# Moving the first attention's output normalisation into its loop, and opening the second projection half on 384 of 512 tokens

## The reference

```python
def per_block(qb):                       # 128 queries; NSA heads
    p_c = masked_softmax(s_c, cmp_end[None, :] <= tq[:, None])   # 31 compressed keys
    p_s = masked_softmax(s_s, ...)       # all selected keys
    p_w = masked_softmax(s_w, m_w)       # window
...
o = g[..., 0:1] * o_c + g[..., 1:2] * o_s + g[..., 2:3] * o_w
o = head_rms_norm(o, out_g.reshape(Hn, D))        # o * rsqrt(mean(o*o) + eps) * g, per head of 64
y_nsa = o.reshape(B, T, NSA_WIDTH) * jax.nn.silu(gate)
...
# memory group: softmax over 256 memory keys, head_rms_norm, silu gate
x = x + concat([y_rwkv, y_nsa, y_mem], -1) @ w_out[l]
```

## Time and profile before

| | |
|---|---|
| median of 3 runs | 1946.72 us |
| profiled execution, its own time | 1947.26 us |
| profiled execution, span | 1945.3 us |
| PE busy | 1828.1 us, 94% |
| DVE busy | 903.6 us, 46% |
| ACT busy | 833.8 us, 43% |
| attention's last value product ends | 484.07 us into the span |
| first matmul of stage_out | 502.88 us |

### The profile page before, as it was taken

The page is one execution under the profiler, slowest core; times in us unless marked ns, Lnnn a source line. Parts: engine busy times, 40 slices in busy tenths (PEclk is TensorE's granted clock), DMA queues, the critical chain, the costliest instruction groups (busy, mean ns, idle before and its releaser), DMA issues. The chain is left out here.

```text
span 1945.3 us, 31456 instructions
## 1 busy us (share of the span) xinstructions
PE 1828.1 (94%) x12576; PEld 1434.1 (74%) x12576; DVE 903.6 (46%) x1638; ACT 833.8 (43%) x1375; POOL 244.5 (13%) x205
## 2 busy tenths in 40 slices
PE   6998999899689899899999999999997999999996
PEld 5776666676566676678888888788886878888885
DVE  2663555544566784443333332564554433333233
ACT  4543444454342445353444322665563253444222
POOL 3011231000124000030000000322220120000000
PEclk9999999899898899999999999999998999999998
DMA  4232000200121000113332333222220223333331
GB/s 181 89 96 66 25 30 29 93 23 1 47 79 33 1 1 1 55 55 101 95 96 96 97 97 98 65 86 73 77 66 23 83 70 97 97 97 97 98 98 44
DMA packets 38486, 133.97 MB, mean 69 GB/s; under 512 B 4896, under 2 KB 5344, under 8 KB 38112
## 3 DMA queue, kind: packets, MB, share of 16 engines
q1 hardware_dynamic: 37504, 130.07, 21.5%
q10 hardware_dynamic: 864, 2.23, 0.3%
HBM read 129.40 MB, written 2.10 MB: 68 GB/s over the span
## 5 line engine op out<-in xcount | busy, mean ns | idle before, releaser
L140 DVE TENSOR_TENSOR big_parts<-ring,big_parts 128x1024 fp32r<-128x1024 f32 x168 | 209.7, 1250 | 530.3 <-ACT big_parts L135 530.3
L166 PE MATMUL bank<-h_parts,big_parts 128*128 128x512 f32 x960 | 381.5, 397 | 10.2 <-DVE big_parts L140 6.5
L168 PE MATMUL bank<-h_parts,big_parts 128*128 128x512 f32 x960 | 375.7, 391 | 0.0
L167 PE MATMUL bank<-y_parts,big_parts 128*128 128x512 f32 x960 | 375.7, 391 | 0.0
L135 ACT ACTIVATE big_parts<-ring 128x1024 fp32r<-128x1024 f32 x168 | 177.9, 1060 | 286.7 <-PE bank L168 285.4
L166 PEld LDWEIGHTS bank<-h_parts,big_parts 128*128 128x128 f32 x960 | 181.1, 189 | 56.8 <-issue 12.5
L168 PEld LDWEIGHTS bank<-h_parts,big_parts 128*128 128x128 f32 x960 | 181.3, 189 | 38.4
L167 PEld LDWEIGHTS bank<-y_parts,big_parts 128*128 128x128 f32 x960 | 181.6, 189 | 36.3
L166 PE MATMUL bank<-h_parts,work_parts 128*128 128x512 f32 x336 | 136.4, 406 | 24.9 <-DVE work_parts L140 23.8
L166 PE MATMUL bank<-big_parts 128*128 128x512 f32 x352 | 136.9, 389 | 0.0
L167 PE MATMUL bank<-work_parts,big_parts 128*128 128x512 f32 x352 | 136.9, 389 | 0.0
(11 more groups left out here) (394 smaller groups left out, 2851.3 us busy)
## 6 DMA issues: line engine op xcount, KB each, us to landing
ring<-in_wstream SPq DMA_DIRECT2D x229, 512.0 KB, 3.6
x<-in_xt SPq DMA_DIRECT2D x8, 512.0 KB, 6.9
out_t<-x SPq DMA_DIRECT2D x8, 256.0 KB, 2.0
work<-in_memt ACTq DMA_DIRECT2D x1, 1024.0 KB, 14.3
y<-in_cw SPq DMA_DIRECT2D x1, 1024.0 KB, 5.1
cst<-in_cst ACTq DMA_DIRECT2D x1, 768.0 KB, 8.2
cos<-in_reset SPq DMA_DIRECT2D x2, 256.0 KB, 6.9
big<-work SPq DMA_DIRECT2D x4, 128.0 KB, 3.8
```

The source lines that it names most:

```text
L140: dve.tensor_tensor(self.parts[:, self.place_of(n), 1, :, :], self.ring[:, n % RING, :, :], self.parts[:, self.place_of(n), 0, :, :].bitca ...
L166: pe.matmul(out, w[0], x[0], start=start, stop=False, skip_group_check=True)
L167: pe.matmul(out, w[0], x[1], start=False, stop=False, skip_group_check=True)
L168: return pe.matmul(out, w[1], x[0], start=False, stop=stop, skip_group_check=True)
```

## The change

A new class `OutTail` takes over what stood behind the loop, in pieces. Its tables give the turn in which each piece stands: block q is squared and summed right after its last group is finished (turns 20, 36, 52; for the last block the memory heads at 64 and the NSA heads behind the loop). One root for blocks 0 to 2 stands in turn 53, reciprocal and the three scalings in turns 54 to 56, turning in 56, 58 and 61 into banks 6, 6 and 7 (those of the value products, hence new waits), gating in 57, 59, 62, casts in 58, 60, 63, differences in 59, 61, 64. The last block follows in two halves. Two slabs are cast ahead, in turns 50 and 65, and the first is split in 51. Behind the loop PE runs output tiles m = 0 and 1 on the first 384 tokens; stage_out does their last 128 tokens and then m = 2 to 7 as before. The parts of the slabs lie in `bigr` throughout.

```diff
@@ stage_nsa
+    head, tail = OutHead(c), OutTail(c, out)
+    def aside(pe, n):
+        head.tensor(pe, n)
+        tail.tensor(pe, at, n)
...
         def _(pe):
             for n in at.turns():
                 at.tensor_turn(pe, n)
-            for q in range(QT):
-                pe.wait_ge(o_sem, 4 + q)
-                for m in range(4):
-                    mm = pe.transpose(c.bank[q][:, m * P:(m + 1) * P],
-                                      out[:, q, 2 * m:2 * m + 2, :].rearrange("p h d -> p (h d)"), con(c, "ident"))
-                mm.then_inc(turned, 1)
+            tail.dense(pe, at, 0)
+            tail.turn_last(pe, at)
+            tail.dense(pe, at, 1)
...
                 at.scalar_turn(act, n)
                 head.scalar(act, n)
-            act.wait_ge(o_sem, 2)
-            act.activation(ssq, ssq, ACT.Sqrt, bias=c.eps[:, 0:1], scale=1.0 / HD).then_inc(root, 1)
+                tail.scalar(act, n)
+            tail.scalar_last(act)
...
-            dve.wait_ge(at.finished, len(finishes))
-            flat = lambda x: x.rearrange("p q (h d) -> p q h d", d=HD)
-            dve.tensor_tensor(flat(sq), out, out, ALU.mult).then_inc(o_sem, 1)
-            dve.wait_ge(o_sem, 1)
-            dve.tensor_reduce(ssq, sq.rearrange("p q (h d) -> p (q h) d", d=HD), AX.X, ALU.add).then_inc(o_sem, 1)
...
+                tail.vector(dve, at, n)
+            tail.vector_last(dve, at)
+class OutTail:
+    ROOTED, CAST = 53, (50, 65)
+    SUMS, SCALED, TURNED, GATED, HIGH, LOW = ({20: 0, 36: 1, 52: 2, 64: 3}, {54: 0, 55: 1, 56: 2, 66: 3}, {56: 0, 58: 1, 61: 2, 67: 3},
+                                              {57: 0, 59: 1, 62: 2}, {58: 0, 60: 1, 63: 2}, {59: 0, 61: 1, 64: 2})
+    BANKS = (6, 6, 7, 5, 3)
+    DONE = (QT - 1) * P
...
+    def tensor(self, pe, at, n):
+        i = self.TURNED.get(n)
+        if i in (0, 1):
+            pe.wait_ge(at.finished, 13)
+            if i:
+                pe.wait_ge(self.gated, 1)
+        elif i == 2:
+            pe.wait_ge(at.finished, 14)
+        elif i == 3:
+            self.c.slab_done_wait(pe, self.slab - 1)
+        if i is not None:
+            self.turn(pe, i)
+        if n == 56 + Attend.SUM:
+            pe.wait_ge(self.gated, 2)
+        elif n == 60 + Attend.SUM:
+            pe.wait_ge(self.gated, 3)
...
+    def dense(self, pe, at, m):
+        c, half, at_q = self.c, KT // 2, slice(0, self.DONE)
+        if m == 0:
+            pe.wait_ge(at.maxed, len(at.units))
+            pe.wait_ge(self.split, 3)
+            c.slab_wait(pe, self.slab)
+        for k in range(half):
+            product(pe, c.bank[m][:, at_q], c.slab_parts(self.slab, m * half + k), (c.hr[:, half + k, at_q], c.yr[:, half + k, at_q]),
+                    k == 0, k == half - 1)
...
+    def scalar(self, act, n):
+        if n in self.HIGH:
+            self.high(act, self.HIGH[n])
+        if n == self.ROOTED:
+            self.root(act, self.ssq[:, 0:8 * (QT - 1)], 3)
+        elif n == 65:
+            self.root(act, self.factors(3), 4)
+        if n in self.CAST:
+            self.c.cast_slab(act, self.slab + self.CAST.index(n))
+    def scalar_last(self, act):
+        self.root(act, self.factors(4), 5)
+        self.high(act, 3)
+        self.high(act, 4)
...
+    def vector_last(self, dve, at):
+        self.sums(dve, at, 4)
+        self.gate(dve, 3)
+        self.invert(dve, self.factors(4), 3)
+        self.scale(dve, 4)
+        self.low(dve, 3)
+        self.gate(dve, 4)
+        self.low(dve, 4)
@@ stage_out
-    c.place_parts(1)
+    c.place_parts(0, c.bigr)
...
+                cols = slice(OutTail.DONE if m < 2 else 0, T)
                 for k in range(half):
-                    if m == 0:
-                        yp.wait(pe, k)
-                    mm = product(pe, c.bank[m][:, :], c.slab_parts(n, m % 2 * half + k), yp.tile(k), k == 0, k == half - 1)
+                    mm = product(pe, c.bank[m][:, cols], c.slab_parts(n, m % 2 * half + k),
+                                 (c.hr[:, half + k, cols], c.yr[:, half + k, cols]), k == 0, k == half - 1)
...
-            c.cast_slab(act, slab)
-            for k in range(half):
-                yp.scalar(act, k)
-            c.cast_slab(act, slab + 1)
```

More of the change, by code:

```diff
@@ L1391, in stage_nsa @@
     out = wk(c, 6272, QT, 8, HD)
-    coef, ssq, o_sem, sq_sem, root, turned = wk(c, 8320, P), wk(c, 8448, QT * 8), *(c.sem(f"na_{n}") for n in
-                                                                                     ("o", "sq", "root", "o_turned"))
-    y_out = c.sem("na_y_out")
+    coef = wk(c, 8320, P)
     tmp = wk(c, 15616, 4, HD)
@@ L1426, in stage_nsa @@
         finishes += [gated(q, 0), gated(q, 1), plain(q), gated(q, 2)]
-    head = OutHead(c)
+    head, tail = OutHead(c), OutTail(c, out)
+    def aside(pe, n):
+        head.tensor(pe, n)
+        tail.tensor(pe, at, n)
     fill = {n: 12 if n == 0 else 1 for n in range(len(units)) if n == 0 or head.turn_of(n + Attend.TURN) is None}
-    at = Attend(c, "na", units, 8576, 4, finishes, fill, (3, 4), head.tensor)
-    sq = wk(c, 8576, QT, 8 * HD)
+    at = Attend(c, "na", units, 8576, 4, finishes, fill, (3, 4), aside)
     with nc.Block() as block:
@@ L1463, in _ @@
                 head.vector(dve, n)
-            dve.wait_ge(at.finished, len(finishes))
-            flat = lambda x: x.rearrange("p q (h d) -> p q h d", d=HD)
-            dve.tensor_tensor(flat(sq), out, out, ALU.mult).then_inc(o_sem, 1)
-            dve.wait_ge(o_sem, 1)
-            dve.tensor_reduce(ssq, sq.rearrange("p q (h d) -> p (q h) d", d=HD), AX.X, ALU.add).then_inc(o_sem, 1)
-            dve.wait_ge(root, 1)
-            dve.reciprocal(ssq, ssq).then_inc(o_sem, 1)
-            dve.wait_ge(o_sem, 3)
@@ L1787, in stage_out @@
     added, made = c.sem("out_added"), c.sem("out_made")
-    norm = Norm(c, tag, c.big, 10, "rms", ("final_g", 0), None, 0)
-    c.place_parts(1)
+    norm = Norm(c, tag, c.big[:, 8:16, :], 10, "rms", ("final_g", 0), None, 0)
+    c.place_parts(0, c.bigr)
     here = c.parts
     c.norm = norm
-    yp = TileParts(c, "out_y", c.y[:, half:KT, :], c.hr[:, half:KT, :], c.yr[:, half:KT, :])
     def next_stage():
@@ L1836, in _ @@
         def _(dve):
[L1837 to L1840, removed]
             c.split_slab(dve, slab + 1)
```

79 lines of the change are left out of this document (added).

## The result

The change takes the kernel from 1946.72 to 1932.06 us (medians of 5 runs each, 1946.28 to 1950.97 and 1930.66 to 1938.25). The ratio is 0.9924, with a 95% interval from 0.9904 to 0.9943: 14.7 us faster. The prediction had the direction, and 8.5 us; the range began at 1934.2, so the time lies 2.1 us outside it. Its two local parts were right to 0.1 us (behind the loop) and 0.8 us (in it), and its sum was wrong by what happens in code that the change does not touch.

A forecast was written before the change was run, and what follows sets the result against it. PE was taken to bound the kernel, with time to be had only where it pauses, behind the loop. 16.5 us won less 8.0 lost gave 8.5 net, hence 1938.2 us; range 1934.2 to 1943.0.

The forecast's parts named there:

- two local parts: Last value product to end of tile 1, 16.5 us won; pieces moved into the attention loop, 8.0 us lost.
- The new tail: From the last value product to the end of tile 1: 5.8 + 0.8 + 2.9 = 9.5 us instead of 26.0.
- the nearest row for the unseen form: Output tiles' 24 matmuls of 128 columns: 0.12 us apart, taken from transposes and 256-column products, 2.9 us in all.
- the rival of dear narrow matmuls: The 24 narrow matmuls cost 0.227 us each instead of 0.12: +2.6 us, total 1940.8; chance 0.18.
- The cost in the loop: Stops of PE from the pieces inserted in the attention loop's turns, summed to 8.0 us.
- turns 51 to 54: Split and sums on DVE, cast on ACT; minimums late, 0.55 and 0.3 come through to PE: 0.85 us.
- the 0.5 for turns 20 and 36: Squares and sums of a block on DVE run into a slab's split; some 0.25 us comes through each time.
- 0.7 us of delay is hidden, the rest stops PE: Attention loop's ring of PE, DVE and ACT: delays of DVE or ACT up to 0.7 us per turn cost nothing.
- no row of PE at 1.2 GHz between 480 and 510: Sign around the loop's end and next stage's start: PE never at half clock there.
- this rival: Pauses in turns 55 to 67 drop PE to half rate before the dense part: about +4.5 us, 1942.7; chance 0.06.
- the first part: From the last value product to the end of tile 1: 9.5 us instead of 26.0, 16.5 us won.
- Behind tile 1 the two kernels do the same work at the same pace: Everything after output tile 1: no difference between the kernels, so the sum ends there.

The follow-up runs named there:

- Tail4: The changed kernel with 4 warm matmuls added behind the attention stage's last dense matmul; 1937.08 us, kernel before 1948.91 in the same measurement.
- after_plus8: The changed kernel with 18 more warm matmuls at the attention loop's fourth turn, 7.8 us of padding; 1942.65 us, ratio to the kernel before 0.9976.
- last: The changed kernel with the second slab's cast moved behind the loop and the last-but-one transposes behind the last value product; 1932.45 us, kernel before 1946.35.
- tail8: The changed kernel with 8 warm matmuls added behind the attention stage's last dense matmul; 1940.88 us, kernel before 1948.91 in the same measurement.
- noload: The changed kernel with Identity instead of Sqrt in turn 53, so two table loads go; 1933.45 us, kernel before 1946.35.
- nodense: The changed kernel without dense matmuls behind the loop, tiles 0 and 1 over all 512 tokens in the next stage; 1937.48 us, kernel before 1946.35.

## Why the prediction was right and wrong

- **The bound** was read rightly: two waits of 15 us and a cold start behind the loop. The new tail measured 9.57 against 9.5, and each part close to its row: 0.11 and 0.17 us apart for 128 and 384 columns, 0.83 for the barrier. The choice of the nearest row for the unseen form (0.12, between 0.06 and 0.227) was right, the rival of dear narrow matmuls is refuted.
- **The cost in the loop** was +7.0 us at full clock against 8.0 forecast, and turn by turn it came where it was named. Tail4's turns less those of the kernel before, beside the forecast: turns 51 to 54 0.7 (0.85), 55 1.7 (1.85), 56 0.8 (0.9), 58 and 61 0.9 (1.05), 60 1.6 (1.5), 65 to 67 1.4 (1.35). The one term that came out at nothing is the 0.5 for turns 20 and 36. The rule "0.7 us of delay is hidden, the rest stops PE" carried.
- **The clock in the loop** was misjudged. The sign that the prediction named held ("no row of PE at 1.2 GHz between 480 and 510"), but the clock fell earlier, behind turn 55. It cost 1.6 us in both profiles of the changed kernel and nothing in the variants. The argument against this rival, that the clock is 1.00 throughout the loop and fell only in the 7.4 us pause, was wrong already for the kernel before: from 366.1 to 372.9 us, in the loop's first turns, its granted clock is 0.50.
- **The step that failed** is in the first part: "Behind tile 1 the two kernels do the same work at the same pace", and with it a difference of nothing ahead of the loop. The work is the same. The pace was not: the rest took 1412.4 us instead of 1418.9, with 75.2 us at 1.2 GHz in it instead of 89.8. The falls that are missing stand behind norms' one-column sums and pauses of about 2 us, which both kernels have; which of them cost a fall depends on when they come. The profiled pair differs by 16.5 us where 8.5 were forecast: 6.5 more behind the stage, 2.5 more upstream, 0.9 less in the parts that were summed. That the 2.5 belong to single runs is shown by the repeats. That the change's instructions do not carry the 6.5 is shown by the profiles of after_plus8, last and tail8, which have them and 0.9 us or none of that gain. What fixes the positions of the falls was not shown.
- **The range** had room for the local terms alone. The spread that a repeat of one kernel shows (1943 to 1954 for the kernel before) was not visible in the three times given, 1946.28 to 1948.31, and none was allowed for. How much of this is the draw of the runs shows in the repeat: there the changed kernel's median was 1937.58, 0.6 us from the forecast and inside the range. That closeness would have been luck, since the same parts were wrong.

Open: whether the gain in the rest is typical of the changed kernel. The group at 1931 to 1933 has it in both profiles. The group at 1938, nearly half of its runs, was never profiled. Its clock of 0.972 is that of the profiled runs of noload, after_plus8 and last, whose rests are 1417.3 to 1419.0, so these runs may lack the gain; that is argued, not shown, since nodense has a rest of 1411.7 at 0.973. Why upstream chance is forgotten by the time the rest begins, so that it repeats to 0.1 us, was not tried either.

## What to carry to other kernels

Measure a change between marks of the same instructions around it, before reading the total: here that separates 7.6 us of the change (9.3 where the loop stays at full clock) from 6.5 of the clock further on. Where PE pauses by 1 to 3 us in many stages, or runs short streams of one-column matmuls, a shift of everything by a few microseconds can be worth as much as an edit, and a forecast of the total needs a range that allows for it. One profile per variant is one draw: take several before a difference far behind the edit is put down to it. And a serial piece is best moved into a loop by handing each queue only what its slack in one turn takes: two moves of steps in the changed kernel's loop were worth 2.5 us.

## What was not expected of the hardware

The same 7542 matmuls kept PE busy for 1343.4 to 1351.7 us, and the length of the program behind the change went with it, 1411.7 to 1419.0 us, while the other engines' busy times stayed within 0.6 us. Per kernel it repeated to 0.1 us (three profiles of one order of instructions, two of the other), although the loop began up to 4.3 us apart in them. The clock fell to half not only behind pauses: at 1226.3 us of the kernel before it fell where PE had been busy without a gap, behind 64 one-column matmuls, and behind the same 64 in the changed kernel it stayed at 1.00. It also fell behind waits of 0.5 and 1.6 us in the loop of the changed kernel, and in the same loop, with turn 52 at 455.2 us or later instead of 451.0 and 452.8, it stayed at full clock.
